# One vector instruction in place of three for the bias and the maximum of a softmax, on one Trainium2 core

## The chip, the core and the metric

The kernel runs on one core of one Trainium2 chip. TensorE (PE) multiplies matrices, VectorE (DVE) and ScalarE (ACT) work on tiles of 128 rows in the on-chip memory (SBUF) and in the eight accumulator banks (PSUM, named `ps` in the rows), GpSimd (POOL) has a small part, and SyncE (SP) starts the loads. Each engine runs its own list of instructions in order; semaphores tie the lists together. The metric is the device time of one execution in microseconds (us).

## The reference, cut to what matters

Two transformer-like blocks over 512 positions, width 1024, in float32. Four kinds of attention in it take a softmax over the scores of a query against its keys; everything else is projections, norms, a recurrence and two MLPs.

```python
def masked_softmax(s, mask):                       # first block, window and selected branches (NSA)
    s = jnp.where(mask, s.astype(jnp.float32), NEG_INF)
    m = jnp.max(s, axis=-1, keepdims=True)
    e = jnp.exp(s - m) * mask
    return e / jnp.maximum(jnp.sum(e, axis=-1, keepdims=True), 1e-30)
...
    s = jnp.einsum('bthd,bmhd->bhtm', q, mem_k) * (MEM_HEAD_DIM ** -0.5)   # memory heads, no mask
    prob = jax.nn.softmax(s.astype(jnp.float32), axis=-1)
```

The second block has differential attention (four heads of two score maps each, with a distance bias whose slope depends on the head), latent attention (four heads, called mla, block-causal mask) and, twice, cross attention to a memory of 256 rows (four heads, no mask). Each is softmax(scale * scores + bias) times values.

## The kernel before, in words

All activations lie transposed, 128 features by 512 positions. `dense` (L189) makes each product of a 128-column weight unit from three passes of float32r halves (`hi`, `lo`); ACT makes the high half of the next weights (`round_unit`, L165), DVE the low half (`rest_unit`, L171). That is most of PE's work.

The order on each engine is written out by hand: every stage is a set of generators, one for PE, one for DVE, one for ACT, and `weave` takes one step of each lane in turn. So the steps of different heads and of the dense products alternate in a fixed order on each engine.

A softmax head runs in steps of 128 queries, called items. In step n:
- PE makes the scores of item n into a bank (one for each of the item's one or two heads), the transposes of the probabilities of item n-1 (L157), and the product with the values of item n-2.
- DVE first finishes item n-1 (`head_vector`: reciprocal L382, gate L385, probabilities scaled L390), then prepares item n: the mask tile of 128 columns is added to the last 128 columns of the scores (L399), the row maximum over all nk columns is taken (L403), and it is multiplied by minus the scale (L406). Between these three DVE waits for its own last result.
- ACT takes the exponential with that column as bias, and sums the row (L421); it also copies the transposed probabilities (L432).

`nsa_heads`, `mem_heads`, `mla_head` and `cross_head` build such heads. NSA: 2 pairs of heads, 8 items each, nk = 128, 256, 384, 512 twice over, two heads in an item. Memory heads: 2 pairs, 4 items, nk = 256. mla: 4 heads, 4 items, nk = 128 to 512. Cross: 2 layers of 4 heads, 4 items, nk = 256. The mla and cross items have one score map each. Differential attention (`diff_vector`, `diff_scalar`) has code of its own: 4 heads, 4 items, two score maps in an item; the bias covers all nk columns, so one instruction for each map adds slope * 8 * dist to the scores (L1611), one takes the maximum (L1615), and one instruction scales both maxima (L1618). Its probabilities are finished by L1597, L1599, L1600 and L1603. The tiles are `db_...` and `dc_...` for its two lanes; lane A beside them runs the mla projections.

Every projection leaves its bank by `evac` (L273): times the row of reciprocal norms R, on DVE.

Of the kernel before, what the change touches and what calls it, by code (L numbers as in the profile page):

```python
# [268 lines left out]
def evac(K, M, v, key, dst, R, m=128):  # L269

    v.wait_ge(*K.done("pe", *key))
    v.wait_ge(*K.own("dve"))
    v.tensor_tensor(dst, K.bank(*key)[0:m, 0:dst.shape[1]], R, ALU.mult).then_inc(  # L273
        *K.tell("dve", *key, frees=key))
# [27 lines left out]
class Heads:  # L302


    def __init__(self, key, items, scale, ready, values, pr, pt, st, diag=None, first=True):
        self.key, self.items, self.scale, self.ready, self.values = key, items, scale, ready, values
        self.pr, self.pt, self.st, self.diag, self.first = pr, pt, st, diag, first
        self.heads = range(len(items[0].prods))
# [852 lines left out]
def nsa_vector(K, M, v):  # L1161
# [34 lines left out]
    weight_lo(K, M, v)  # L1196
    evac(K, M, v, ("gl",), s.tmp[0:12, :], R[0:12, :], 12)
# [70 lines left out]
def nsa_heads(M, z):  # L1268
# [6 lines left out]
    for br, k in enumerate((s.ks, s.kw)):  # L1275
        for i in range(4):
# [5 lines left out]
                 diag=M.C("causal"), first=False)  # L1282
# [64 lines left out]
def mem_heads(M, z):  # L1347
# [5 lines left out]
    return Heads(("memh", z), items, 0.125, [("dve", "mq", z)], [("act", *M0, "vt", 1)], s.pr, s.pt, s.st)  # L1353
# [230 lines left out]
def diff_vector(K, M, v, h, L):  # L1584
    k = ("df", h)
    for n, dst in (("q", L.q), ("k", L.k), ("v", L.sq)):
        project(K, M, v, (*k, n), dst)
        yield
    slope = 2.0 ** (-8.0 * (h + 1) / 4)
    if h < 2:  # L1590
        v.wait_ge(*K.landed("cs", 4))
    for step in range(6):
# [13 lines left out]
        if i < 4:  # L1606
            nk, st = (i + 1) * 128, L.st[i % 2]
            v.wait_ge(*K.done("pe", *k, "s", i, 1))
            for z in range(2):
                b = K.bank(*k, "s", i, z)  # L1610
                v.scalar_tensor_tensor(out=b[:, 0:nk], in0=M.even.dist(i), scalar=slope * 8.0, in1=b[:, 0:nk],  # L1611
                                       op0=ALU.mult, op1=ALU.add).then_inc(*K.tell("dve", *k, "bias", i, z))
            v.wait_ge(*K.own("dve"))
            for z in range(2):
                v.tensor_reduce(st[:, z:z + 1], K.bank(*k, "s", i, z)[:, 0:nk], AX, ALU.max).then_inc(  # L1615
                    *K.tell("dve", *k, "max", i, z))
            v.wait_ge(*K.own("dve"))
            v.tensor_scalar(st[:, 6:8], st[:, 0:2], -0.125, None, ALU.mult).then_inc(*K.tell("dve", *k, "nmax", i))  # L1618
# [11 lines left out]
def diff_scalar(K, M, a, h, L):  # L1630
# [5 lines left out]
    for step in range(6):  # L1636
        i = step
        if i < 4:
# [173 lines left out]
def mla_head(M, h, L):  # L1812
# [8 lines left out]
                 [("act", "ukv", h, "t")], [[x] for x in L.pr], [[x] for x in L.pt], L.st, diag=s.cm)  # L1821
# [31 lines left out]
def cross_head(M, n, h, L):  # L1853
# [3 lines left out]
    return Heads(("xh", n, h), items, 1.0 / 16, [("dve", "xq", n, h, 1), ("dve", "m", n + 1, "k", 2 * h + 1)],  # L1857
# [10 lines left out]
def queries_vector(K, M, v, n, h, fresh=None):  # L1868
    for z in range(2):
# [3 lines left out]
        evac(K, M, v, ("xq", n, h, z), M.Y[2 * h + z], M.R)  # L1873
# [356 lines left out]
def sync_program(K, M, s, dram):  # L2230

    load(K, s, "cst", M.pv, dram["pvec"])
    for n, (name, u) in enumerate(K.units):
# [27 lines left out]
        if (name, u) == ("w_out", 5):  # L2261
# [4 lines left out]
            load(K, s, "cs", M.even.cm, dram["cmask"])  # L2266
# [17 lines left out]
def build(nc, dram):  # L2284
    with ExitStack() as ctx:
# [48 lines left out]
        def pair_tiles(name, n, g_at, xf, s4, y, stats, after=None):  # L2334
# [25 lines left out]
                                          tile("cmp_w2", 42), tile("cmp_mask", 43))  # L2360
        s.q, s.qr = tiles("nsa_q", plain(1, 0), 2), tiles("nsa_qr", plain(1, 2), 2)
# [17 lines left out]
        s.cm = tile("cmask", 23)[:, 0:128]  # L2379
# [200 lines left out]
```

## Time and profile before

| what | us |
|---|---|
| median of 3 runs | 2209.06 (2205.78 to 2210.96) |
| the profiled execution, its time | 2210.41 |
| its span | 2209.1 |
| PE busy | 2049.4 |
| DVE busy | 1126.6 |
| ACT busy | 872.0 |

The span is the time from the first to the last instruction of the profile. Busy is the time in which an engine had at least one instruction under way, so two that overlap count once. The granted clock of PE over the span was 0.96 of full speed. The first block lies at 0 to 550 us (NSA and memory heads from 138 to 290), differential and latent attention from 555 to 780, the two cross layers around 845 to 965 and 1685 to 1803; the rest is dense work.

### The profile page before, as it was taken

What the parts mean: (1) busy time and instruction counts of PE and PEld (TensorE: products, weight loads), DVE (VectorE), ACT (ScalarE), POOL (GpSimd) and SP (SyncE); (2) the same over time, 40 slices, a digit from 0 to 9 for tenths busy, and PEclk for the clock granted to TensorE, in tenths of its full rate; (3) what the DMA queues carried; (4) which work ended last, traced back from release to release, by engine and by line L of the source; (5) the groups of instructions that cost most, each with busy time, mean ns of one, the idle gap of its engine ahead of it and who ended that gap; (6) DMA issues with size and microseconds to landing.
All of it is one profiled execution on the core that took longest, in us unless ns stands there. A gap on an engine that the chain in (4) does not pass through costs nothing.

```text
span 2209.1 us, 28369 instructions
## 1 busy us (share of the span) xinstructions
PE 2049.4 (93%) x11400; PEld 1622.4 (73%) x11400; DVE 1126.6 (51%) x2014; ACT 872.0 (39%) x1567; POOL 27.2 (1%) x68
## 2 busy tenths in 40 slices
PE   6888888899988999999999999999989999999997
PEld 5765666677756578978888887677567978888886
DVE  5666468737466455445343345344455445443344
ACT  5325443245343444434232233465644344232232
POOL 0000000000000000000000000011100000000000
PEclk9989899999989799999999999999999999999999
DMA  5210011012211023212222222111123312222321
GB/s 197 86 48 21 20 48 58 3 59 99 86 41 56 1 96 115 96 62 95 101 96 96 101 92 95 58 58 48 39 77 105 108 64 96 96 100 91 105 94 69
DMA packets 52051, 169.64 MB, mean 77 GB/s; under 512 B 5776, under 2 KB 9424, under 8 KB 51920
## 3 DMA queue, kind: packets, MB, share of 16 engines
q1 hardware_dynamic: 51920, 167.82, 21.7%
q8 instruction: 92, 1.51, 0.3%
q14 instruction: 39, 0.32, 0.0%
HBM read 165.70 MB, written 2.10 MB: 76 GB/s over the span
## 4 chain that ended last, share of the span: by engine, by line
PE 63%; DVE 3%; ACT 2%; issue 1%; POOL 0%; DVEq 0%; ACTq 0%
PE ps L152 62%; PE ps L157 1%; DVE X L1523 0%; DVE st L403 0%; DVE macc L233 0%; ACT sa_sp L2103 0%; DVE x_pr L390 0%; ACT sb_sp L2103 0%; ACT msq L226 0%; ACT sa_sp L2106 0%; ACT sa_sp L2101 0%; ACT sb_sp L2106 0%; ACT sb_sp L2101 0%; DVE lo L1431 0%; DVE st L1615 0%
## 5 line engine op out<-in xcount | busy, mean ns | idle before, releaser
L152 PE MATMUL ps<-hi,wr 128*128 128x512 f32 (+1 forms) x4616 | 1407.7, 385 | 50.7 <-DVE wr L171 34.3
L152 PEld LDWEIGHTS ps<-hi,wr 128*128 128x128 f32 x4616 | 862.4, 190 | 230.7 <-DVE wr L171 25.7
L152 PE MATMUL ps<-lo,wr 128*128 128x512 f32 (+1 forms) x2308 | 880.4, 381 | 0.0
L152 PEld LDWEIGHTS ps<-lo,wr 128*128 128x128 f32 x2308 | 440.0, 191 | 84.5 <-issue 3.9
L165 ACT ACTIVATE wr<-raw 128x1024 fp32r<-128x1024 f32 x293 | 307.7, 1052 | 349.3 <-PE ps L152 349.3
L171 DVE TENSOR_TENSOR wr<-raw,wr 128x1024 fp32r<-128x1024 f32 x293 | 356.7, 1217 | 4.3 <-ACT wr L165 2.3
L1450 DVE TENSOR_TENSOR X<-X,ps 128x512 f32<-128x512 f32 x96 | 66.0, 687 | 238.1 <-PE ps L152 238.1
L1986 ACT ACTIVATE mlp<-mlp 128x512 f32<-128x512 f32 x64 | 40.4, 632 | 207.8 <-DVE mlp L1969 207.8
L1969 DVE SCALAR_TENSOR_TENSOR mlp<-ps,R 128x512 f32<-128x512 f32 x64 | 44.2, 691 | 113.2 <-PE ps L152 106.2
L213 ACT ACTIVATE hi<-X,pv 128x512 fp32r<-128x512 f32 x48 | 34.7, 722 | 138.4 <-DVE X L1450 135.9
L1972 DVE TENSOR_TENSOR lo<-mlp,hi 128x512 fp32r<-128x512 f32 x64 | 44.3, 692 | 87.8 <-ACT hi L1990 87.8
L218 DVE SCALAR_TENSOR_TENSOR lo<-X,pv,hi 128x512 fp32r<-128x512 f32 x48 | 36.0, 751 | 40.7 <-ACT hi L213 40.7
L403 DVE TENSOR_REDUCE st<-ps 128x1 f32<-128x256 f32 (+3 forms) x96 | 41.7, 455 | 13.9 <-PE ps L152 10.1
L421 ACT ACTIVATE x_pr<-ps,st 128x256 f32<-128x256 f32 x32 | 15.2, 474 | 68.0 <-DVE st L406 68.0
L226 ACT ACTIVATE sq<-X 128x512 f32<-128x512 f32 x49 | 30.3, 619 | 28.9 <-DVE X L1450 28.9
L1990 ACT ACTIVATE hi<-mlp 128x512 fp32r<-128x512 f32 x64 | 40.4, 632 | 2.7 <-ACT mlp L1986 0.4
L233 DVE TENSOR_TENSOR acc<-acc,sq 128x512 f32<-128x512 f32 x50 | 34.6, 693 | 10.0 <-ACT sq L226 5.6
L273 DVE TENSOR_TENSOR Y<-ps,R 128x512 f32<-128x512 f32 x16 | 11.1, 691 | 54.3 <-PE ps L152 47.0
L152 PE MATMUL ps<-x_pt,vt 128*128 128x128 f32 x256 | 34.3, 277 | 2.9 <-ACT x_pt L432 2.9
L152 PEld LDWEIGHTS ps<-x_pt,vt 128*128 128x128 f32 x256 | 32.3, 191 | 5.4 <-ACT x_pt L432 4.6
L152 PE MATMUL ps<-sa_sp,cst 128*128 128x128 f32 (+3 forms) x84 | 27.3, 468 | 6.8 <-POOL sa_sp L2125 6.8
L152 PE MATMUL ps<-kt,Y 128*128 128x256 f32 x128 | 32.6, 379 | 0.0
(694 smaller groups left out, 1912.6 us busy)
## 6 DMA issues: line engine op xcount, KB each, us to landing
raw<-d_w SPq DMA_DIRECT2D x128, 512.0 KB, 3.4
raw<-d_wkv SPq DMA_DIRECT2D x32, 512.0 KB, 3.4
raw<-d_w_in SPq DMA_DIRECT2D x30, 512.0 KB, 3.5
raw<-d_sb_w_in SPq DMA_DIRECT2D x24, 512.0 KB, 3.4
raw<-d_ev_w_in SPq DMA_DIRECT2D x16, 512.0 KB, 3.5
raw<-d_wq SPq DMA_DIRECT2D x16, 512.0 KB, 3.4
raw<-d_wo SPq DMA_DIRECT2D x16, 512.0 KB, 3.5
X<-d_xT SPq DMA_DIRECT2D x16, 256.0 KB, 5.1
```

What stands on the lines that cost most here:

```text
L152: return pe.matmul(out, lhsT, rhs, start=start, stop=stop, skip_group_check=True)
L165: a.activation(M.wr[u % 3][:, 0:1024], M.raw[u % 4], ACT.Copy).then_inc(*K.tell("act", "hi", u))
L171: v.tensor_tensor(w[:, 1024:2048], M.raw[u % 4], w[:, 0:1024].bitcast(F32), ALU.subtract).then_inc(*K.tell("dve", "lo", u))
L213: a.activation(hi, src, ACT.Copy, scale=gcol).then_inc(*K.tell("act", *name, "hi", i))
L218: v.scalar_tensor_tensor(out=lo, in0=src, scalar=gcol, in1=hi.bitcast(F32), op0=ALU.mult, op1=ALU.subtract).then_inc(*K.tell("dve", *name, ...
L233: v.tensor_tensor(acc, acc, tmp[i % 2], ALU.add).then_inc(*K.tell("dve", *name, "sum", i))
L403: v.tensor_reduce(st[:, hh:hh + 1], K.bank(*h.key, "s", n, hh)[:, 0:nk], AX, ALU.max).then_inc(*K.tell("dve", *h.key, "max", n, hh))
L1450: v.tensor_tensor(M.X[u], M.X[u], K.bank(*key, u), ALU.add).then_inc(*K.tell("dve", *key, u, frees=(*key, u)))
L1969: v.scalar_tensor_tensor(out=t, in0=K.bank(*key), scalar=0.0, in1=M.R, op0=ALU.max, op1=ALU.mult).then_inc(*K.tell("dve", *key, frees=key))
L1972: v.tensor_tensor(lo[u], t, hi[u].bitcast(F32), ALU.subtract).then_inc(*K.tell("dve", "h", n, q, "lo", u))
L1986: a.activation(t, t, ACT.Square).then_inc(*K.tell("act", *key, "sq"))
L1990: a.activation(hi[u], t, ACT.Copy).then_inc(*K.tell("act", "h", n, q, "hi", u))
```

## The change

For masked and biased scores the three instructions become one call, `tensor_tensor_reduce`: it adds the mask to the scores, multiplies by minus the scale, writes that back to the bank, and gives the minimum of the row, which is the negated maximum of the scaled scores. The exponential then reads the bank with scale -1. The mask has to cover all nk columns, so the 128 columns of the mask get 384 columns of zeros in front. For NSA that tile is put where the rotation's cosines were, after their last use. In differential attention the slope is taken out of the bias: the queries leave their bank multiplied by 0.125 / slope, and the call scales by -slope. Where there is no mask, the maximum is taken with its sign turned, and the queries leave their bank already scaled.

```diff
-def evac(K, M, v, key, dst, R, m=128):
+def evac(K, M, v, key, dst, R, m=128, scale=None):
...
+    if scale is not None:
+        v.scalar_tensor_tensor(out=dst, in0=K.bank(*key)[0:m, 0:dst.shape[1]], scalar=scale, in1=R, op0=ALU.mult,
+                               op1=ALU.mult).then_inc(*K.tell("dve", *key, frees=key))
+        return
...
+def masked_max(K, v, b, mask, scale, nmax, *key):
+
+    v.tensor_tensor_reduce(out=b, in0=b, in1=mask, scale=-scale, scalar=3e38, op0=ALU.add, op1=ALU.min,
+                           accum_out=nmax).then_inc(*K.tell("dve", *key))
...
             for hh in h.heads:
-                b = K.bank(*h.key, "s", n, hh)
-                if h.diag is not None:
-                    v.tensor_tensor(b[:, nk - 128:nk], b[:, nk - 128:nk], h.diag, ALU.add).then_inc(
-                        *K.tell("dve", *h.key, "diag", n, hh))
-            v.wait_ge(*K.own("dve"))
-            for hh in h.heads:
-                v.tensor_reduce(st[:, hh:hh + 1], K.bank(*h.key, "s", n, hh)[:, 0:nk], AX, ALU.max).then_inc(
-                    *K.tell("dve", *h.key, "max", n, hh))
-            v.wait_ge(*K.own("dve"))
-            v.tensor_scalar(st[:, 2:2 + w], st[:, 0:w], -h.scale, None, ALU.mult).then_inc(
-                *K.tell("dve", *h.key, "nmax", n))
+                b, nmax = K.bank(*h.key, "s", n, hh)[:, 0:nk], st[:, 2 + hh:3 + hh]
+                if h.mask is not None:
+                    masked_max(K, v, b, h.mask[:, T - nk:T], h.scale, nmax, *h.key, "nmax", n)
+                else:
+                    v.tensor_reduce(nmax, b, AX, ALU.max, negate=True).then_inc(*K.tell("dve", *h.key, "nmax", n))
...
+    v.memset(s.mask[:, 0:384], 0.0).then_inc(*K.tell("dve", "mask0"))
+    v.tensor_copy(s.mask[:, 384:T], M.C("causal")).then_inc(*K.tell("dve", "mask"))
...
-    evac(K, M, v, ("mq", z), s.q, M.first.R)
+    evac(K, M, v, ("mq", z), s.q, M.first.R, scale=0.125)
...
             for z in range(2):
-                b = K.bank(*k, "s", i, z)
-                v.scalar_tensor_tensor(out=b[:, 0:nk], in0=M.even.dist(i), scalar=slope * 8.0, in1=b[:, 0:nk],
-                                       op0=ALU.mult, op1=ALU.add).then_inc(*K.tell("dve", *k, "bias", i, z))
-            v.wait_ge(*K.own("dve"))
-            for z in range(2):
-                v.tensor_reduce(st[:, z:z + 1], K.bank(*k, "s", i, z)[:, 0:nk], AX, ALU.max).then_inc(
-                    *K.tell("dve", *k, "max", i, z))
-            v.wait_ge(*K.own("dve"))
-            v.tensor_scalar(st[:, 6:8], st[:, 0:2], -0.125, None, ALU.mult).then_inc(*K.tell("dve", *k, "nmax", i))
+                masked_max(K, v, K.bank(*k, "s", i, z)[:, 0:nk], M.even.dist(i), slope, st[:, 6 + z:7 + z], *k, "nmax", i)
...
+    v.memset(s.cm[:, 0:384], 0.0).then_inc(*K.tell("dve", "cm0"))
```

On DVE, at the last item (nk = 512) of lane db in the second pair of differential heads, the order before was this. `ps` is a bank with scores, `dist_287` the distances, `st` the columns of statistics.

```order
L1611 SCALAR_TENSOR_TENSOR ps<-dist_287,ps 128x512 [waits s_pe]
L1611 SCALAR_TENSOR_TENSOR ps<-dist_287,ps 128x512
L1615 TENSOR_REDUCE st<-ps 128x1 [waits s_dve]
L1615 TENSOR_REDUCE st<-ps 128x1
L1618 TENSOR_SCALAR st<-st 128x2 [waits s_dve]
```

And now, with the finishing of the other lane's item behind it. An `ISA` row that reads a bank is the new instruction; the `ISA` row with one column behind it writes out the minimum that it gathered.

```order
L380 ISA ps,st<-ps,dist_287 128x512 [waits s_pe]
L380 ISA st 128x1
L380 ISA ps,st<-ps,dist_287 128x512
L380 ISA st 128x1
L1604 RECIPROCAL st<-st 128x2 [waits s_act]
L1606 TENSOR_TENSOR st<-st,omm 128x1 [waits s_dve]
L1607 TENSOR_SCALAR dc_pr_317<-dc_pr_317,st 128x384
L1610 SCALAR_TENSOR_TENSOR dc_pr_317<-dc_p_316,st,dc_pr_317 128x384 [waits s_dve]
```

Five instructions with two waits of DVE for itself became four without such a wait; what follows them, up to the probabilities that PE waits for, stands as it did.

At the first three mla items on DVE, with `cmask` as the mask tile, the order before was:

```order
L399 TENSOR_TENSOR ps<-ps,cmask 128x128 [waits s_pe]
L403 TENSOR_REDUCE st<-ps 128x1 [waits s_dve]
L406 TENSOR_SCALAR st<-st 128x1 [waits s_dve]
L399 TENSOR_TENSOR ps<-ps,cmask 128x128 [waits s_pe]
L403 TENSOR_REDUCE st<-ps 128x1 [waits s_dve]
L406 TENSOR_SCALAR st<-st 128x1 [waits s_dve]
```

And now:

```order
L380 ISA ps,st<-ps,cmask 128x128 [waits s_pe]
L380 ISA st 128x1
L380 ISA ps,st<-ps,cmask 128x128 [waits s_pe]
L380 ISA st 128x1
L380 ISA ps,st<-ps,cmask 128x128 [waits s_pe]
L380 ISA st 128x1
```

Three instructions became two. The order on PE is the same row for row, and on ACT too but for the line numbers. In the whole program there are 80 such pairs, 20 each of nk = 128, 256, 384 and 512.

## Rows read from the trace of the kernel before

**Rows 1.** The page: busy us of each engine, share, instructions.

```profile
PE 2049.4 (93%) x11400; PEld 1622.4 (73%) x11400; DVE 1126.6 (51%) x2014; ACT 872.0 (39%) x1567; POOL 27.2 (1%) x68
```

**Rows 2.** What PE waited for, 138 to 292 us: total us, times, longest.

```profile
PE ps L157 <- DVE mem_pr L390: 8.0, 5, 3.9
PE ps L152 <- ACT nsa_pta L432: 3.9, 2, 3.3
PE ps L157 <- DVE nsa_pra L390: 3.7, 4, 1.9
```

**Rows 3.** What PE waited for, whole span, same columns.

```profile
PE ps L157 <- DVE dc_pr L1603: 7.3, 7, 1.8
...
PE ps L157 <- DVE db_pr L1603: 4.5, 3, 2.8
...
PE ps L152 <- ACT x_pt L432: 2.9, 6, 0.5
...
PE ps L157 <- DVE mla_pr L390: 2.1, 3, 1.2
```

**Rows 4.** Groups by form, DVE: busy us, mean ns, idle before.

```profile
L1611 DVE SCALAR_TENSOR_TENSOR ps<-dist,ps 128x512 f32<-128x512 f32 x8 | 5.2, 690 | 1.7 <-PE ps L152 1.7
L273 DVE TENSOR_TENSOR Y<-ps,R 128x512 f32<-128x512 f32 x16 | 11.1, 691 | 54.3 <-PE ps L152 47.0 <-ACT R L256 7.0
```

**Rows 5.** Timeline of DVE, differential items nk = 128 and 512: start, us.

```profile
604.28 0.48 DVE L1611 SCALAR_TENSOR_TENSOR ps<-dist,ps 128x128 f32<-128x128 f32 x2
604.80 0.49 DVE L1615 TENSOR_REDUCE st<-ps 128x1 f32<-128x128 f32 x2
605.32 0.17 DVE L1618 TENSOR_SCALAR st<-st 128x2 f32<-128x2 f32 x1
...
708.79 1.29 DVE L1611 SCALAR_TENSOR_TENSOR ps<-dist,ps 128x512 f32<-128x512 f32 x2 [1.67 <-PE ps L152]
710.12 1.29 DVE L1615 TENSOR_REDUCE st<-ps 128x1 f32<-128x512 f32 x2
711.44 0.17 DVE L1618 TENSOR_SCALAR st<-st 128x2 f32<-128x2 f32 x1
```

**Rows 6.** The same view, an NSA item with nk = 512.

```profile
280.85 0.49 DVE L399 TENSOR_TENSOR ps<-ps,cst 128x128 f32<-128x128 f32 x2
281.37 1.29 DVE L403 TENSOR_REDUCE st<-ps 128x1 f32<-128x512 f32 x2
282.69 0.17 DVE L406 TENSOR_SCALAR st<-st 128x2 f32<-128x2 f32 x1
```

**Rows 7.** The same view, mla item nk = 128, and the next one's start.

```profile
727.26 0.29 DVE L399 TENSOR_TENSOR ps<-ps,cmask 128x128 f32<-128x128 f32 x1
...
727.99 0.29 DVE L399 TENSOR_TENSOR ps<-ps,cmask 128x128 f32<-128x128 f32 x1
```

**Rows 8.** Timeline of ACT: an exponential with its sum, and the next.

```profile
702.73 0.58 ACT L1646 ACTIVATE db_pr<-ps,st 128x384 f32<-128x384 f32 x1 [2.23 <-DVE st L1597]
703.20 0.19 ACT L1646 ACTIVATION_READ_ACCUMULATOR db_pr<-ps,st 128x1 f32 x1
703.30 0.57 ACT L1646 ACTIVATE db_p<-ps,st 128x384 f32<-128x384 f32 x1
```

**Rows 9.** Timeline of PE, waits (in brackets) in the first differential pair.

```profile
625.50 0.66 PE L157 MATMUL ps<-cst,db_pr 128*128 128x128 f32 x2 [2.82 <-DVE db_pr L1603]
...
637.95 0.52 PE L157 MATMUL ps<-cst,dc_pr 128*128 128x128 f32 x3 [1.75 <-DVE dc_pr L1603]
...
642.78 0.63 PE L157 MATMUL ps<-cst,db_pr 128*128 128x128 f32 x4 [2.26 <-DVE st L1597]
```

**Rows 10.** Stretches: us, busy PE PEld DVE ACT POOL, PE clock, DMA.

```profile
630.00:640.00 10.00, 7.63 (x36) 4.76 (x35) 9.72 (x22) 4.76 (x12) 0.00 (x0) 0.95 0.16 55
...
730.00:740.00 10.00, 10.00 (x21) 4.63 (x21) 5.02 (x20) 2.94 (x13) 0.00 (x0) 0.50 0.00 0
```

**Rows 11.** Groups by line: loads of ACT's function table.

```profile
L248 ACT ACT_TABLE_LOAD x7 | 9.0, 1283 | 2.5 <-PE ps L152 2.4
```

More of the change, by code:

```diff
@@ L302, with __init__ @@
 class Heads:
-    def __init__(self, key, items, scale, ready, values, pr, pt, st, diag=None, first=True):
+    def __init__(self, key, items, scale, ready, values, pr, pt, st, mask=None, first=True):
         self.key, self.items, self.scale, self.ready, self.values = key, items, scale, ready, values
-        self.pr, self.pt, self.st, self.diag, self.first = pr, pt, st, diag, first
+        self.pr, self.pt, self.st, self.mask, self.first = pr, pt, st, mask, first
         self.heads = range(len(items[0].prods))
@@ L421, in head_scalar @@
                 a.activation(h.place(h.pr, n, hh), K.bank(*h.key, "s", n, hh)[:, 0:nk], ACT.Exp,
-                             bias=st[:, 2 + hh:3 + hh], scale=h.scale, accum_out=st[:, 4 + hh:5 + hh]).then_inc(
+                             bias=st[:, 2 + hh:3 + hh], scale=1.0 if h.mask is None else -1.0, accum_out=st[:, 4 + hh:5 + hh]).then_inc(
                     *K.tell("act", *h.key, "e", n, hh, frees=(*h.key, "s", n, hh)))
@@ L1281, in nsa_heads @@
     return Heads(("nsa", z), items, 0.125, [("dve", "kw", "rope")], [("act", "vsw", "t")], s.pr, s.pt, s.st,
-                 diag=M.C("causal"), first=False)
+                 mask=s.mask, first=False)
 def nsa_heads_tensor(K, M, pe, z):
@@ L1352, in mem_heads @@
              for i in range(4)]
-    return Heads(("memh", z), items, 0.125, [("dve", "mq", z)], [("act", *M0, "vt", 1)], s.pr, s.pt, s.st)
+    return Heads(("memh", z), items, 1.0, [("dve", "mq", z)], [("act", *M0, "vt", 1)], s.pr, s.pt, s.st)
 def mem_heads_tensor(K, M, pe, z):
@@ L1524, in scale_vector, with project @@
                            op1=ALU.mult).then_inc(*K.tell("dve", *name, "x", i))
-def project(K, M, v, key, dst):
+def project(K, M, v, key, dst, scale=None):
     weight_lo(K, M, v)
@@ L1533, in project @@
         factors_vector(K, M, v)
-    evac(K, M, v, key, dst, M.R)
+    evac(K, M, v, key, dst, M.R, scale=scale)
 def diff_tensor(K, M, pe, h, L):
@@ L1585, in diff_vector @@
     k = ("df", h)
-    for n, dst in (("q", L.q), ("k", L.k), ("v", L.sq)):
-        project(K, M, v, (*k, n), dst)
+    slope = 2.0 ** (-8.0 * (h + 1) / 4)
+    for n, dst, scale in (("q", L.q, 0.125 / slope), ("k", L.k, None), ("v", L.sq, None)):
+        project(K, M, v, (*k, n), dst, scale)
         yield
-    slope = 2.0 ** (-8.0 * (h + 1) / 4)
     if h < 2:
@@ L1646, in diff_scalar @@
                 a.activation(pr[:, 0:nk], K.bank(*k, "s", i, z)[:, 0:nk], ACT.Exp, bias=st[:, 6 + z:7 + z],
-                             scale=0.125, accum_out=st[:, 2 + z:3 + z]).then_inc(
+                             scale=-1.0, accum_out=st[:, 2 + z:3 + z]).then_inc(
                     *K.tell("act", *k, "e", i, z, frees=(*k, "s", i, z)))
@@ L1820, in mla_head @@
     return Heads(("ml", h), items, 192.0 ** -0.5, [("act", "ukn", h), ("dve", "qrp", h // 2, "rope")],
-                 [("act", "ukv", h, "t")], [[x] for x in L.pr], [[x] for x in L.pt], L.st, diag=s.cm)
+                 [("act", "ukv", h, "t")], [[x] for x in L.pr], [[x] for x in L.pt], L.st, mask=s.cm)
 def mla_head_tensor(K, M, pe, h, L):
@@ L1856, in cross_head @@
                   [[(("xo", n, h, z), 0, lambda j, z=z: s.vap(j, 2 * h + z)) for z in range(2)]]) for i in range(4)]
-    return Heads(("xh", n, h), items, 1.0 / 16, [("dve", "xq", n, h, 1), ("dve", "m", n + 1, "k", 2 * h + 1)],
+    return Heads(("xh", n, h), items, 1.0, [("dve", "xq", n, h, 1), ("dve", "m", n + 1, "k", 2 * h + 1)],
                  [("act", "m", n + 1, "vt", 2 * h + 1)], [[x] for x in L.pr], [[x] for x in L.pt], L.st)
@@ L1872, in queries_vector @@
             v.wait_ge(*K.done("act", *fresh, "R"))
-        evac(K, M, v, ("xq", n, h, z), M.Y[2 * h + z], M.R)
+        evac(K, M, v, ("xq", n, h, z), M.Y[2 * h + z], M.R, scale=1.0 / 16)
 def queries_scalar(K, M, a, n, h, fresh=None):
@@ L2265, in sync_program @@
                 load(K, s, "cs", M.even.dist_t[j][:, 0:w], dram["dist"][:, j * T:j * T + w])
-            load(K, s, "cs", M.even.cm, dram["cmask"])
+            load(K, s, "cs", M.even.cm[:, 384:T], dram["cmask"])
             load(K, s, "mcs", M.even.cos, dram["mla_cos"])
@@ L2360, in build @@
                                           tile("cmp_w2", 42), tile("cmp_mask", 43))
+        s.mask = s.cos
         s.q, s.qr = tiles("nsa_q", plain(1, 0), 2), tiles("nsa_qr", plain(1, 2), 2)
@@ L2378, in build @@
         s.dist = lambda i: (d[0][:, 0:128], d[2][:, 0:256], d[0][:, 128:512], d[1])[i]
-        s.cm = tile("cmask", 23)[:, 0:128]
+        s.cm = tile("cmask", 23)
         s.cos, s.sin, s.kr, s.kn, s.vn = (tile("mla_cos", 24), tile("mla_sin", 25), tile("mla_kr", 26),
```

## The prediction

> **What bounds the kernel now.** I read the busy line of the page first, then what PE waited for, then DVE's timeline at those places. PE is busy 2049.4 of 2209.1 us, DVE 1126.6 [rows 1]. So DVE's time is worth nothing by itself; it counts where PE stands and waits for it, within some 160 us of idle PE in all. The reader is to look for waits that end at a softmax tile. In the stretch of NSA and memory heads these are `mem_pr` (8.0 us), `nsa_pra` (3.7) and, with ACT as the last link, `nsa_pta` (3.9) [rows 2]. In the differential and latent stages they are `dc_pr` (7.3), `db_pr` (4.5) and `mla_pr` (2.1); in cross attention only `x_pt` (2.9, six waits) [rows 3]. From 630 to 640 us DVE is busy 9.72 of 10 while PE is idle 2.4 [rows 10]: there DVE sets the pace.
>
> **The change on DVE, part by part.** The new instruction is in no row of before, so it is priced from its nearest relatives. The pass itself reads a bank and an SBUF tile and writes the bank, as L1611 does: 690 ns at 512 columns [rows 4]. Writing out the gathered minimum is a second instruction, as the order shows. ACT does the same kind of thing behind an exponential: the read-out takes 0.19, but it starts 0.47 after an activation of 0.58, and the next activation starts 0.57 after the first [rows 8]. So it costs the queue next to nothing between two passes, and its end comes 0.08 after the pass before it. I take a pass at its full length, and 0.08 once behind the last.
>
> Differential items (16). At nk = 512 the five instructions run from 708.79 to 711.61, 2.82 us [rows 5]. Two passes and a tail are 2 x 0.69 + 0.08 = 1.46: 1.36 less. At nk = 128 they run from 604.28 to 605.49, 1.21 [rows 5]; two passes of 0.29 and the tail are 0.66 (0.29 is the mask add of 128 columns, [rows 7]): 0.55 less. Four equally spaced sizes average 0.955, so 16 items give 15.3 us.
>
> NSA items (16). At nk = 512: 280.85 to 282.86, 2.01 [rows 6], against 1.46: 0.55 less. The mask add was 128 columns wide at every size, and is now as wide as the row, but rides in the pass of the maximum; so the difference is the same at every size: 8.8 us.
>
> mla items (16). From one item's start to the next one's at nk = 128 are 0.73 us [rows 7]; now 0.29 + 0.08 = 0.37. 0.36 less each: 5.8 us.
>
> Unmasked items (8 memory, 32 cross). The scaling of the maximum goes: 0.17 long in [rows 5, 6]. The next instruction can start before its end, as the second exponential does in [rows 8], so some 0.11 of it is queue time: 4.4 us for 40. A maximum with turned sign I take at the price of one without.
>
> Added: two memsets of 384 columns and a copy of 128. None can cost more than the 0.69 of a 512 column pass [rows 4], so at most 2.1; I take 1.0. The 22 projections that now multiply twice (4 differential, 2 memory, 16 cross queries) become the kind of instruction that L1611 is, 690 against 691 ns [rows 4]: nothing. The load of the mla mask moves the same bytes.
>
> Together DVE gets 15.3 + 8.8 + 5.8 + 4.4 - 1.0 = 33 us less to do.
>
> **What of it reaches the end.** Differential stage: DVE's order in a round is finish db, prepare db, finish dc, prepare dc. PE's wait for `dc_pr` stands behind the preparation of db in the same round, so it shrinks by up to 1.36: the wait of 1.75 at 637.95 falls to 0.4 [rows 9]. Then `db_pr` at 642.78 (2.26) stands behind the preparation of dc; it falls to about 0.9. The wait of 2.82 at 625.50 does not count: the projections for mla and their norm on ACT come directly before it on DVE. So of 7.3 + 4.5 + 2.3 = 14.1 us [rows 3, 9] 11.3 are open to the change, of which I take 80%, 9 us. Waits that end at ACT, in the same chains, give some 2 more. Sum 11, of 15.3 saved.
>
> NSA and memory stage: the three waits of [rows 2] sum to 15.6. PE steps of the recurrence lie between, and the memory items lose only their scaling. I take 5 of the 8.8 + 0.9, by the rule that DVE is busy somewhat over half of that stretch.
>
> mla: three items stand in a row behind each other from 727.26; 3 x 0.36 = 1.1. Then PE runs at half clock from 730 on, fully busy [rows 10], and hides the rest until near 758; the last head alone, where each item is a chain PE, DVE, ACT, DVE, PE, gives 4 to 5 x 0.36. Sum 3, near the 2.1 that PE waits for `mla_pr` and the ACT waits beside it.
>
> Cross: an exponential that starts some 0.15 earlier shortens a part of six waits of 2.9 in all: 0.7. The memsets and the copy: -0.5, where DVE is ahead of PE.
>
> Sum: 11 + 5 + 3 + 0.7 - 0.5 = 19 us. The profiled execution took 2210.4; it would be 2191. The median of before lies 1.3 lower, so the prediction is 2190.
>
> **The clock.** In [rows 10] PE's granted clock is 0.95 where it waits often but briefly and 0.50 (1.2 GHz) at 730 to 740, after waits at 700 to 730. Ten us at that level do the work of five. Shorter waits may keep such a stretch at 2.4 GHz, or the shifted waits may bring one down that was up. I hold one stretch of some 20 us either way for possible: 10 us. That gives the likeliest case its own range, 2180 to 2200.
>
> The Trainium skill, Vector Engine (DVE) Microarchitecture Reference, "Points that are easy to get wrong", warns of a related instruction: with two SBUF sources that aren't bf16 its rate is halved, since no read port is left for the accumulator. Here one source is a bank, so the rule as written would not strike; if it held for this instruction as well, the time would be that of the rival named half rate.
>
> **The rivals.**
>
> Half rate. If gathering the minimum takes a second cycle for each column, the length-dependent part of a pass doubles. From 0.29 and 0.69 at 128 and 512 columns a column costs 1.04 ns; passes become 0.42 and 1.22. A differential item is then 0.92 to 2.52 (0.3 less than before), an NSA item 0.92 to 2.52 against 1.23 to 2.01 (0.1 more on average), an mla item about equal. DVE saves 7 or 8 us, the path 3: 2206. For it: a gathered result is fed back each cycle; against it: L403 gathers too, at 1.29 for two passes of 512 [rows 6], the full rate. Chance 0.14.
>
> The gain goes elsewhere. ACT's exponentials and the recurrence's steps become the last link in most waits, so that only half of the 19 us arrives: 2200. For it: `nsa_pta` and the ACT waits [rows 2]; against it: the exponential itself waits for the column that now comes earlier. Chance 0.17.
>
> A fixed price for the new instruction. DVE has not run this operation before; if changing between it and the ordinary ones costs a setup, 80 pairs pay it. The nearest row is ACT's load of a function table, 1283 ns [rows 11]: 80 x 1.28 = 103 us more on DVE, 69 more net of the 33 saved, some 55% of it on the path: 2248. It breaks even at 33 / 80 = 0.42 us for each pair; from there on the kernel is slower than before. Against it: none of DVE's own operation changes in [rows 5 to 7] shows a gap over 0.04 us. Chance 0.06.
>
> It does what it says: the order shows the three instructions gone at all 88 items, so that is no rival.
>
> **How the numbers follow.** The forecast has 0.63 (2180 to 2200), the others 0.14, 0.17 and 0.06. The range reaches over the two small-gain cases to 2207, and down to 2179 for a clock that gains a whole stretch. A measurement of this kernel tells 0.2%, 4.4 us, from no change. Faster by more than that: the forecast nearly whole (0.61), the third case nearly whole (0.15), 0.03 of the half rate: 0.79. Within: 0.12, mostly half rate. Slower: 0.09, the fixed price and a clock that falls while the gain is small.
>
> **What would show it.** In the profile after: the new pass at 512 columns near 690 ns (1.2 us would be half rate; over 1.1 at 128 columns the fixed price); two passes and their read-outs at the place of 708.79 in some 1.5 us; DVE busy 1126.6 - 33 = 1094; waits for `dc_pr` and `db_pr` down from 11.8 to about 3; those for `mem_pr` almost as before; PE busy up or down with the clock alone. If DVE's busy time falls as said and the waits move to ACT rows, the third case was right. If the time falls by much more than 25 us, the clock did it, and a stretch such as 730 to 750 stands at 1.00.

## The result, and the profile after

| | median of 4 runs, us | range |
|---|---|---|
| before, run beside it | 2207.42 | 2205.06 to 2210.96 |
| after | 2168.78 | 2164.83 to 2172.61 |

The ratio is 0.9831, 95% interval 0.9808 to 0.9853: 38.6 us faster. The forecast was 19 us, and the range began at 2179. The direction was right, the size half of what came. Both profiled executions, before's and after's, took 3 to 4 us longer than their medians, so the two are fairly compared.

The page of after, its span and its busy line, answers to [rows 1]. The profiled execution took 2172.6.

```profile
span 2171.4 us, 28244 instructions
PE 2030.9 (94%) x11400; PEld 1613.2 (74%) x11400; DVE 1088.7 (50%) x1929; ACT 873.4 (40%) x1567; POOL 27.3 (1%) x68
```

The first thing to read here is a subtraction. PE idle was 2209.1 - 2049.4 = 159.7 and is 2171.4 - 2030.9 = 140.5: 19.2 us less, which is the sum of waits that was forecast. The other 18.5 us are PE's *busy* time, with the same 11400 instructions in the same order. What differs beside it is the granted clock, 0.960 over the span of before and 0.970 over that of after; that it is the cause is what the experiments have to show. DVE is 37.9 less busy (33 forecast); ACT stands as it was.

The groups of DVE by form, columns as in [rows 4]: the new instruction, its read-out, the maximum with turned sign, and the projection that now multiplies twice.

```profile
L412 DVE TENSOR_REDUCE st<-ps 128x1 f32<-128x256 f32 x48 | 19.6, 422 | 12.2 <-PE ps L152 11.9
L380 DVE DVE_READ_ACCUMULATOR2_ANT st<- 128x1 f32 x80 | 11.3, 142 | 0.0
L274 DVE SCALAR_TENSOR_TENSOR Y<-ps,R 128x512 f32<-128x512 f32 x16 | 11.1, 692 | 55.2 <-PE ps L152 47.9 <-ACT R L256 7.0
L380 DVE CUSTOM_DVE_ANT_0 ps<-ps,dist 128x512 f32<-128x512 f32 x8 | 5.4, 713 | 0.8 <-PE ps L152 0.8
...
L380 DVE CUSTOM_DVE_ANT_0 ps<-ps,dist 128x128 f32<-128x128 f32 x8 | 2.2, 315 | 1.1 <-PE ps L152 1.1
```

The pass takes 713 ns at 512 columns and 315 at 128, so 1.04 ns for a column, as an ordinary one, and some 25 ns more in all. There is no second cycle for a column (half rate would be 1220) and no fixed price (that would show at 128).

DVE's timeline at the place of 708.79 in [rows 5], the differential item with nk = 512:

```profile
686.03 0.70 DVE L380 CUSTOM_DVE_ANT_0 ps<-ps,dist 128x512 f32<-128x512 f32 x1 [0.76 <-PE ps L152]
686.65 0.14 DVE L380 DVE_READ_ACCUMULATOR2_ANT st<- 128x1 f32 x1
686.65 0.73 DVE L380 CUSTOM_DVE_ANT_0 ps<-ps,dist 128x512 f32<-128x512 f32 x1
687.30 0.14 DVE L380 DVE_READ_ACCUMULATOR2_ANT st<- 128x1 f32 x1
687.30 0.16 DVE L1604 RECIPROCAL st<-st 128x2 f32<-128x2 f32 x1
```

Each read-out starts together with the next instruction, so it takes nothing from the queue. The last column is there 687.44 - 686.03 = 1.41 us after the start (2.82 before, 1.46 forecast), and the next instruction starts after 1.27.

What PE waited for, whole span, columns as in [rows 2]:

```profile
PE ps L157 <- DVE mem_pr L401: 7.2, 3, 3.9
PE ps L157 <- DVE db_pr L1610: 3.7, 2, 2.6
PE ps L152 <- ACT nsa_pta L437: 3.5, 2, 2.7
PE ps L157 <- DVE nsa_pra L401: 2.9, 4, 1.2
...
PE ps L152 <- ACT x_pt L437: 2.6, 6, 0.5
PE ps L157 <- DVE dc_pr L1610: 2.5, 6, 0.7
```

Against [rows 2, 3], `dc_pr` fell from 7.3 to 2.5, and `db_pr` from 4.5 to 3.7. What is left of the latter is mostly the wait of 2.82 in [rows 9] that the prediction left out; it is on PE's timeline of after as

```profile
613.48 0.41 PE L157 MATMUL ps<-cst,db_pr 128*128 128x128 f32 x2 [2.64 <-DVE db_pr L1610]
```

**Where the other half came from.** Lined up by the 293 instructions of L171, one for each weight unit, after is ahead by 9.2 us at 300 us, 11.1 at 606, 17.1 at 649 and 39.5 at 784; from there to the end the lead stays between 37.5 and 40.2. So 22 us of the 38 were won in the second differential pair and in mla. The stretches there, columns as in [rows 10], before:

```profile
690.00:700.00 10.00, 7.13 (x38) 4.41 (x36) 8.20 (x33) 6.29 (x24) 0.00 (x0) 1.00 0.14 52
700.00:710.00 10.00, 7.43 (x27) 3.80 (x27) 7.69 (x20) 4.00 (x13) 0.00 (x0) 0.80 0.01 2
710.00:720.00 10.00, 8.25 (x47) 5.84 (x46) 8.22 (x21) 5.61 (x15) 0.00 (x0) 0.85 0.01 2
720.00:730.00 10.00, 8.83 (x47) 6.11 (x46) 5.30 (x16) 7.12 (x17) 0.00 (x0) 1.00 0.01 2
...
740.00:750.00 10.00, 10.00 (x19) 4.20 (x18) 2.94 (x10) 2.09 (x7) 0.00 (x0) 0.50 0.00 0
```

and after:

```profile
690.00:700.00 10.00, 9.51 (x62) 7.63 (x60) 4.43 (x10) 8.15 (x17) 0.00 (x0) 1.00 0.00 1
700.00:710.00 10.00, 10.00 (x40) 5.23 (x40) 6.19 (x27) 5.70 (x21) 0.00 (x0) 1.00 0.01 2
710.00:720.00 10.00, 10.00 (x37) 4.41 (x35) 4.15 (x16) 4.21 (x12) 0.00 (x0) 1.00 0.00 1
720.00:730.00 10.00, 9.79 (x73) 8.32 (x72) 3.59 (x14) 5.64 (x13) 0.00 (x0) 1.00 0.01 2
```

Two more stretches belong here, first of before and then of after, in the first differential pair:

```profile
620.00:630.00 10.00, 6.91 (x19) 3.49 (x19) 6.91 (x18) 4.22 (x13) 0.00 (x0) 0.50 0.00 1
```

```profile
620.00:630.00 10.00, 8.87 (x57) 6.95 (x56) 8.06 (x23) 5.95 (x14) 0.00 (x0) 1.00 0.03 9
```

The reader is to see the long stretch at 0.50 (1.2 GHz) in the first table, 20 us with PE 10.00 busy, together with its 730 to 740 in [rows 10], and that the same latent products at 700 to 720 of after stand at 1.00. On PE's timelines one pair of them, first before, then after:

```profile
735.04 1.49 PE L152 MATMUL ps<-mla_kn,Y 128*128 128x384 f32 x2
```

```profile
705.90 0.81 PE L152 MATMUL ps<-mla_kn,Y 128*128 128x384 f32 x2
```

### The profile page after: what moved, and what is told of

Same layout as the page of the kernel before. It is cut to its first block, busy times and chain, and to the rows that moved or that the text cites. A ratio compares the mean times of both kernels' runs of the same rounds, so it can differ in the third digit from the quotient of the medians.

```text
span 2171.4 us, 28244 instructions
## 1 busy us (share of the span) xinstructions
PE 2030.9 (94%) x11400; PEld 1613.2 (74%) x11400; DVE 1088.7 (50%) x1929; ACT 873.4 (40%) x1567; POOL 27.3 (1%) x68
## 4 chain that ended last, share of the span: by engine, by line
PE 85%; DVE 9%; ACT 4%; issue 1%; DMA 0%; POOL 0%; SPq 0%; DVEq 0%; ACTq 0%
PE ps L152 83%; PE ps L157 3%; DVE ps L380 1%; DVE wr L171 1%; DVE X L1530 0%; DVE lo L218 0%; DMA cst<-d_cst 0%; DVE macc L233 0%; DVE ra_S L769 0%; DVE rc_S L769 0%; DVE rb_S L769 0%; DVE ra_Z L789 0%; ACT sa_sp L2103 0%; DVE x_acc L233 0%; ACT wr L165 0%
## 5 line engine op out<-in xcount | busy, mean ns | idle before, releaser
L171 DVE TENSOR_TENSOR wr<-raw,wr 128x1024 fp32r<-128x1024 f32 x293 | 356.7, 1217 | 4.3 <-ACT wr L165 2.3
L274 DVE SCALAR_TENSOR_TENSOR Y<-ps,R 128x512 f32<-128x512 f32 x16 | 11.1, 692 | 55.2 <-PE ps L152 47.9
L152 PEld LDWEIGHTS ps<-x_pt,vt 128*128 128x128 f32 x256 | 32.3, 191 | 5.2 <-ACT x_pt L437 4.3
L152 PE MATMUL ps<-sb_sp,cst 128*128 128x128 f32 (+3 forms) x84 | 26.8, 455 | 7.5 <-POOL sb_sp L2125 7.5
```

The lines of the kernel that those rows point to most:

```text
L152: return pe.matmul(out, lhsT, rhs, start=start, stop=stop, skip_group_check=True)
L171: v.tensor_tensor(w[:, 1024:2048], M.raw[u % 4], w[:, 0:1024].bitcast(F32), ALU.subtract).then_inc(*K.tell("dve", "lo", u))
```

## The experiments

Each kernel is told as a difference from before or after. A is the theory that the clock gave the half that was not forecast, because PE stood for shorter times ahead of it; what the other letters stand for is in the expectations. "Gain" is the difference of medians to before, run on the same chip: 2206.81 for the first four, 2206.56 for the next four, 2208.98 for the last four. PE idle and PE busy are those of one profiled execution.

| kernel | median (range, runs) | ratio (95%) | gain | PE idle | PE busy |
|---|---|---|---|---|---|
| before | | | | 159.7 | 2049.4 |
| e1_diff_only | 2190.36 (2179.75 to 2199.63, 6) | 0.9925 (0.9897 to 0.9954) | 16.5 | 148.1 | 2039.2 |
| e2_nsa_only | 2200.06 (2194.36 to 2202.51, 11) | 0.9966 (0.9954 to 0.9979) | 6.8 | 155.3 | 2039.8 |
| e3_mla_only | 2195.32 (2193.41 to 2199.28, 5) | 0.9952 (0.9934 to 0.9970) | 11.5 | 155.7 | 2036.4 |
| e4_plain_only | 2209.65 (2201.64 to 2213.25, 12) | 1.0013 (0.9999 to 1.0026) | -2.8 | 155.7 | 2044.7 |
| e5_warm_before | 2201.12 (2195.61 to 2203.36, 8) | 0.9968 (0.9956 to 0.9981) | 5.4 | 157.4 | 2036.9 |
| e6_late_pair | 2173.79 (2172.25 to 2179.91, 4) | 0.9857 (0.9840 to 0.9874) | 32.8 | 144.0 | 2028.3 |
| e7_no_mla | 2174.29 (2168.86 to 2189.17, 6) | 0.9868 (0.9844 to 0.9891) | 32.3 | 143.5 | 2024.1 |
| e9_after_warm | 2167.91 (2166.70 to 2169.73, 4) | 0.9826 (0.9811 to 0.9840) | 38.7 | 133.7 | 2031.8 |
| e10_no_diff | 2189.13 (2181.92 to 2190.47, 5) | 0.9909 (0.9894 to 0.9924) | 19.9 | 152.4 | 2028.3 |
| e11_no_nsa | 2180.24 (2177.32 to 2183.03, 4) | 0.9871 (0.9856 to 0.9886) | 28.7 | 143.1 | 2036.6 |
| e12_masked_only | 2171.63 (2168.30 to 2175.57, 4) | 0.9833 (0.9815 to 0.9851) | 37.4 | 141.0 | 2033.3 |
| e13_after_again | 2169.97 (2165.78 to 2174.12, 4) | 0.9825 (0.9807 to 0.9843) | 39.0 | 139.0 | 2033.9 |

The last two columns need care. The profiled execution was the fastest of its kernel in e3, e4, e5, e7, e9 and e10, by up to 8 us below the median (e4, 2201.64), and that of before was a slow one. What such a pair differs by over the whole span is therefore partly chance. It is safer to compare a stage with the same stage. These are the lengths of three stages in each profile, cut at the same instructions of L171 (which stand at 123, 298, 590, 649, 689 and 784 us in before), and for the third its PE idle time and its granted clock:

| kernel | NSA and memory | first differential pair | second pair and mla | PE idle in it | clock in it |
|---|---|---|---|---|---|
| before | 174.4 | 58.9 | 95.4 | 13.6 | 0.82 |
| e2_nsa_only | 163.0 | 58.9 | 95.4 | 13.6 | 0.82 |
| e4_plain_only | 171.1 | 59.0 | 89.6 | 13.5 | 0.87 |
| e1_diff_only | 174.3 | 51.9 | 76.8 | 8.5 | 0.95 |
| e7_no_mla | 162.6 | 51.3 | 76.7 | 8.5 | 0.95 |
| e3_mla_only | 172.8 | 58.9 | 81.5 | 11.3 | 0.94 |
| e10_no_diff | 160.1 | 58.4 | 81.5 | 11.2 | 0.94 |
| e5_warm_before | 170.4 | 58.9 | 86.3 | 11.3 | 0.94 |
| e6_late_pair | 162.8 | 51.4 | 81.5 | 10.3 | 0.92 |
| after | 165.2 | 51.9 | 73.0 | 6.0 | 0.97 |
| e13_after_again | 162.7 | 52.0 | 74.6 | 6.0 | 0.96 |
| e12_masked_only | 163.9 | 52.1 | 74.5 | 6.0 | 0.96 |
| e11_no_nsa | 173.4 | 52.4 | 73.0 | 6.0 | 0.98 |
| e9_after_warm | 163.9 | 51.6 | 73.0 | 6.0 | 0.98 |

The rest, from 784 us to 2150, takes 1364.8 to 1369.6 in all of them, 1366.1 in before and 1367.8 in after: nothing was won there.

### Each part alone

The edit is before, with the changed lines taken over for one of four parts: differential heads, NSA heads, mla heads, or the heads without a mask ("plain": memory and cross).

```diff
-NEW = ()
+NEW = ("diff",)      # e1; e2 ("nsa",), e3 ("mla",), e4 ("plain",)
```

> Of the change only the differential heads (16 items, scaled queries for them); all other softmaxes as before. Theory A (the waits of PE got shorter by the 19 us forecast, and because PE stood less, its granted clock stayed at 2.4 GHz in stretches where it had been at 1.2, which gave another 19): this part holds the stretch before latent attention, where most of the clock was lost, so it gives 10 us in waits and 10 to 14 in clock, 20 to 25 us less than before, and the half-clock stretch that lay at 730 to 754 us is gone or much shorter. Rival B (every us saved on DVE brings its share, whatever the place: 38.6 us in all for 33 us of DVE): 15.3 us of DVE give 18 less.

> Of the change only the NSA heads (16 items) with their wide mask. A: 8 to 9 us less than before, 4 of it in waits and 4 to 5 in clock (half-clock stretches between 240 and 290 us shorter); nothing later changes. B: 8.8 us of DVE give 10 less. The two hardly differ here; the share of PE busy time in it does: 4 or 5 us less busy by A, none by B.

> Of the change only the latent attention heads (16 items). A: the waits before 730 us stay as they were, so PE still falls to 1.2 GHz there and hides what DVE saves up to 754 us; 2 to 3 us less than before. B: 5.8 us of DVE give 7 less.

> Of the change only the unmasked heads (memory and cross, 40 items): maximum with turned sign, no scaling behind it, scaled queries. A: 0 to 2 us less, since cross attention waits little. B: 4.4 us of DVE give 5 less.

PE idle fell by 11.6, 4.4, 4.0 and 4.0 over the whole span. In the stages that a part changes it fell by 10.8 (e1, both pairs), 4.5 (e2) and 2.3 (e3), against the terms 11, 5 and 3 of the sum. The plain part was forecast at 0.7, and its median shows no gain at all. The gains in time are uneven: 16.5, 6.8, 11.5 and -2.8, in all 32 of the 38. B, a fixed price for each us of DVE, had said 18, 10, 7 and 5; A had said 20 to 25, 8 to 9, 2 to 3 and 0 to 2. Neither fits: 5.6 us less on DVE brought 11.5 (e3), and 7.4 less brought nothing (e4).

mla alone is the surprise: 11.5 us for a term of 3. Its stretches, columns as above:

```profile
700.00:710.00 10.00, 8.50 (x26) 4.18 (x27) 8.05 (x20) 4.53 (x16) 0.00 (x0) 0.66 0.00 0
...
730.00:740.00 10.00, 10.00 (x39) 4.79 (x40) 4.56 (x17) 4.00 (x12) 0.00 (x0) 1.00 0.00 0
740.00:750.00 10.00, 10.00 (x75) 8.24 (x74) 3.20 (x12) 5.84 (x12) 0.00 (x0) 1.00 0.01 2
```

The differential waits up to 710 are still there. The 0.66 at 700 to 710 is the short stretch that before shows as 0.80 and 0.85 from 700 to 720, since e3 runs 3.3 us ahead here. But 730 to 750 now stands at 1.00 instead of 0.50. One wait ahead of it is gone. It is this one, on PE's timeline of before, at the first mla item, directly where its stretch at 0.50 begins:

```profile
717.17 0.63 PE L157 MATMUL ps<-cst,db_pr 128*128 128x128 f32 x4 [1.40 <-ACT dc_p L1646]
718.84 0.63 PE L157 MATMUL ps<-cst,dc_pr 128*128 128x128 f32 x4 [0.35 <-DVE dc_pr L1603]
729.96 0.47 PE L157 MATMUL ps<-cst,mla_pr 128*128 128x128 f32 x1 [1.17 <-DVE mla_pr L390]
```

In e3 the first two are as they were, and no wait stands at the third. In e1 it is the other way round: the wait of 1.40 is gone, the two of 1.6 for `dc_pr` ahead of it are under 0.5, and the third stands, with 1.00 behind it:

```profile
714.31 0.33 PE L158 MATMUL ps<-cst,mla_pr 128*128 128x128 f32 x1 [1.17 <-DVE mla_pr L402]
```

Over all kernels the pattern is this. Where the wait of 1.17 and the differential waits ahead of it both stand (before, e2, e4), the latent products run partly or wholly at a lower level: 0.50 twice over in before and in e2 (720 to 740), 0.74 in e4. Where the differential waits are shorter and the 1.17 stands (e1, e7), or the other way round (e3, e10, e6), or both are short (after and the rest), or the waits are filled (e5), they stand at 1.00: eleven profiles of fourteen. So either part saves this stretch, and both save it once. The stage from 689 to 784 gives the size: the differential part alone shortens it by 18.6 us, mla alone by 13.8, both together by 22.3. The 10.1 us by which the two exceed the whole are what can be won only once. The size is not fixed, though: e4 changes nothing in this stage, has the same waits as before, and came out 5.8 us shorter, with 0.74 in place of 0.50. The expectation of 2 to 3 us under A was wrong, though the means is A's: it had counted the clock for the differential part alone.

### Products that only keep PE busy, in the kernel before

No line of DVE is touched. Where PE would stand and wait for probabilities, it first makes products of a constant tile, whose result nobody reads: 8, 8, 6 and 6 of them at four places (the first two items of the differential head 3, the last item of head 2, and the first mla item). They are work added to the kernel, 28 products of 128 columns, which the trace shows as two instructions each.

```diff
+def warm(M, pe, b, n):
+    for _ in range(n):
+        mm(pe, b[:, 0:128], M.C("ones"), M.C("ones"), True, True)
...
+            warm(M, pe, b, {(3, 0): 8, (3, 1): 8, (2, 3): 6}.get((h, i), 0))
```

> The kernel before, with 28 extra products of 128x128 on PE, whose results nothing reads, where PE waits for probabilities between 692 and 730 us (heads 2 and 3 of differential attention, first item of latent attention). No vector or scalar instruction changes. A (the clock): PE keeps 2.4 GHz where it had 1.2 at 706 to 713 and 730 to 754 us, that is 31 us at half speed less, so the time falls by 10 to 15 us to 2192 to 2197, minus 1 or 2 for products that don't fit into the waits, and PE's instructions of the old kinds there take less time in all. C (the gain beyond the waits is something else, such as less traffic of DVE on the banks): the half-clock stretch may move, but the time stays or rises by 1 to 4 us.

It is 5.4 us *faster* than before, ratio 0.9968 (0.9956 to 0.9981), where C had said the same or slower and A 10 to 15 faster. The granted clock rose with it: on average 0.967 over its eight executions, 0.962 over the thirteen of before beside them. One of the four places on PE's timeline, and the stretches:

```profile
720.63 1.60 PE L152 MATMUL ps<-cst 128*128 128x128 f32 x12
```

```profile
700.00:710.00 10.00, 7.50 (x48) 5.56 (x47) 9.02 (x22) 5.05 (x14) 0.00 (x0) 1.00 0.00 1
710.00:720.00 10.00, 10.00 (x61) 7.68 (x59) 3.98 (x9) 7.04 (x13) 0.00 (x0) 1.00 0.01 2
...
730.00:740.00 10.00, 10.00 (x40) 4.91 (x40) 5.84 (x18) 4.13 (x12) 0.00 (x0) 1.00 0.01 2
740.00:750.00 10.00, 9.08 (x67) 7.49 (x65) 4.07 (x16) 5.20 (x11) 0.00 (x0) 1.00 0.00 0
750.00:760.00 10.00, 7.72 (x31) 4.90 (x31) 3.83 (x13) 3.43 (x10) 0.00 (x0) 0.81 0.00 0
```

DVE does as much as before (1127.0 busy), PE does more, and 730 to 750 stands at 1.00. The place in the row above is that of the wait of 1.17. This is the run that shows the clock as a cause by itself. Over the whole span PE is busy 12.5 us less, but this was the fastest execution of the eight, and 7.9 us of its lead were there at 590 us, before the first filler. The stage with the fillers is the fair measure: 86.3 us instead of 95.4, so 9.0 shorter, 2.3 of it in idle time and 6.7 in PE busy, though the fillers themselves are busy for 7.3. Part of the 9.0 is lost again later, and the clock falls in another place instead (0.81 at 750 to 760).

### Giving back some of DVE's time, in the kernel after

After the new instruction, in the second pair of differential heads alone, DVE waits for itself once and reads both rows again; the result goes to a column that nobody reads.

```diff
                 masked_max(K, v, K.bank(*k, "s", i, z)[:, 0:nk], M.even.dist(i), slope, st[:, 6 + z:7 + z], *k, "nmax", i)
+            if h >= 2:
+                v.wait_ge(*K.own("dve"))
+                for z in range(2):
+                    v.tensor_reduce(st[:, z:z + 1], K.bank(*k, "s", i, z)[:, 0:nk], AX, ALU.max).then_inc(
+                        *K.tell("dve", *k, "nmax", i))
```

> The changed kernel, with DVE's old time put back in the second pair of differential heads alone: after the new instruction it waits for itself and takes the maximum of both maps again, 2.8 us an item at 512 columns as before, before ACT may go on. A: the waits of 690 to 720 come back, 5 or 6 us, and with them part of the half-clock stretch; since latent attention keeps its shorter items, between 5 and 18 us slower than the changed kernel, and the profile's half-clock time at 660 to 770 says which. B (each us of DVE counts alike): 7.7 us of DVE bring 9 us back.

It is 5.0 us slower than after (2173.79 against 2168.78; 5.8 when each is taken against its own before), which is at the low end of what A said and below what B said. DVE's timeline at one such item shows that the delay was really there:

```profile
686.21 0.73 DVE L380 CUSTOM_DVE_ANT_0 ps<-ps,dist 128x512 f32<-128x512 f32 x1
686.86 0.14 DVE L380 DVE_READ_ACCUMULATOR2_ANT st<- 128x1 f32 x1
687.03 1.29 DVE L1621 TENSOR_REDUCE st<-ps 128x1 f32<-128x512 f32 x2
```

DVE is 7.4 busier and PE idle 3.5 more. PE busy over the whole span is not more (2028.3 against 2030.9), but that hides what happened in the stage itself:

```profile
670.00:680.00 10.00, 7.63 (x30) 4.25 (x28) 7.88 (x30) 4.82 (x18) 0.00 (x0) 0.83 0.01 2
680.00:690.00 10.00, 8.41 (x24) 4.12 (x25) 8.09 (x23) 4.69 (x16) 0.00 (x0) 0.66 0.00 0
```

In after both stretches stand at 1.00. So behind the lengthened waits the clock did fall, for some 10 us, and the stage takes 81.5 instead of 73.0, half of the difference in idle and half in busy time. What did not come back is the long stretch in the latent products, which stand at 1.00 from 700 to 730: mla's wait of 1.17 is still gone here. The other stages of this profile happened to run faster than after's, so the total doesn't tell A from B.

### Each part left out of the kernel after

```diff
-NEW = ("nsa", "mla", "diff", "plain")
+NEW = ("nsa", "diff", "plain")      # e7; e10 without "diff", e11 without "nsa", e12 without "plain"
```

> The changed kernel with latent attention as before. Alone that part brought 11 us. A: the half-clock stretch at 730 us goes as soon as either the differential part or this one shortens the waits before it, so its 10 us are counted once; without this part the changed kernel loses only its waits, 3 to 5 us. B (the parts add up): it loses 11 us, or 17 with the 6 us by which the four parts alone fell short of the whole.

> The changed kernel with the differential heads as before. A (19 us of waits, the rest from PE's clock, which a stretch gives back once): this part holds 10 to 12 us of waits, plus the clock of its own two stages, less what latent attention alone keeps up at 730 us; 14 to 20 us slower than the changed kernel. B (time goes with DVE's work): 15.3 of 33 us, 18 slower.

> The changed kernel with the NSA heads as before. Alone the part brought 6 to 7 us, 3 of it in waits. Its stage lies 300 us ahead of the others, so nothing is shared with them. A: 6 to 9 us slower than the changed kernel. B: 10.

> The changed kernel with the unmasked heads as before. Alone that part made the kernel 3 us slower, within its spread, by clock and not by waits. A: the clock of single stretches falls one way or the other with shifts of less than a us, so 3 us to either side of the changed kernel. D (scaled queries and the sign turned cost something): 3 us or more faster than it. B: 5 slower.

> The changed kernel itself once more, beside the three that leave out a part, for direct comparison: 36 to 40 us less than before, and a spread of its runs of 5 to 8 us that goes with their mean granted clock.

The median of after is 2169.97 in the last of these, 2168.78 in its first measurement. Against the one on the same chip, leaving out the differential part costs 19.2 us, NSA 10.3, the plain part 1.7; leaving out mla costs 5.5 against 2168.78. The sum is 37. So mla is worth 11.5 alone and 5.5 as the last one in (6.3 when e7 and after are each taken against their own before): the stretch at 730 to 750 can be saved once, by it or by the differential part, as the pattern above says. A had said 3 to 5, B 11. One of e7's six executions took 2189.17, at a granted clock of 0.961 where the others have 0.969 or more. The 19.2 fits both theories. NSA goes the other way, 6.8 alone and 10.3 as the last one in, nearer to B's 10 than to A's 6 to 9; its stage takes 160.1 to 165.2 us with the change and 170.4 to 174.4 without, so it is worth some 10 us with 4 or 5 us of chance about it. The plain part can't be told from nothing in either setting.

### Filler products in the kernel after

The same helper, with 62 products at seven waits that were left: 36 at three memory items, 6 at an NSA item, 20 at three items of the first differential pair.

```diff
+            warm(M, pe, b, {(0, 1): 10, (0, 0): 6, (1, 0): 4}.get((h, i), 0))
```

> The changed kernel with extra 128x128 products on PE in waits of its own: memory heads items 0 to 2 of the first pair (36), the first item of the second NSA pair (6), first items of differential heads 0 and 1 (20). A: the half-clock stretches at 143 to 160, 249 to 259 and 593 to 617 us shrink, 5 to 10 us less than the changed kernel. C: 0 to 5 us slower, since products that outlast a wait are paid for.

At 2167.91 it is 0.9 below one measurement of after and 2.1 below the other, inside what two measurements of after differ by (1.2) and their ranges. PE idle fell by 6.8, and PE busy rose by 0.9 against the first profile. A had said 5 to 10 us faster, C the same or slower. The granted clock did rise, to 0.977 on average over the four executions from 0.972 over the eight of after, and the time stayed: the fillers, busy for 15.6 us, cost about what their clock gives. No version clearly beats the changed kernel.

## Why the prediction was half right

- **The price of the pass** (0.69, with 0.08 behind the last): right; 0.71, and the item of 512 columns takes 1.41 instead of 1.46. DVE's saving of 33 us was 37.9. By the parts alone (e1 to e4) DVE's busy time fell by 15.0, 8.3, 5.6 and 7.4, against 15.3, 8.8, 5.8 and 4.4: the term that was too small is that of the unmasked items, whose scaling of 0.17 was counted at 0.11. A smaller thing is the overlap of the new passes. The first mla items follow each other on DVE's timeline like this, 0.21 to 0.25 apart and not 0.37:

```profile
701.64 0.29 DVE L380 CUSTOM_DVE_ANT_0 ps<-ps,cmask 128x128 f32<-128x128 f32 x1
701.85 0.14 DVE L380 DVE_READ_ACCUMULATOR2_ANT st<- 128x1 f32 x1
701.85 0.33 DVE L380 CUSTOM_DVE_ANT_0 ps<-ps,cmask 128x128 f32<-128x128 f32 x1
702.10 0.14 DVE L380 DVE_READ_ACCUMULATOR2_ANT st<- 128x1 f32 x1
```

- **What of it reaches the end** (11 + 5 + 3 + 0.7 - 0.5 = 19): right in the sum, 19.2 of PE idle, and in its parts where they were run alone, 10.8, 4.5 and 2.3 in their own stages. `dc_pr` and `db_pr` came to 6.2 and not "about 3", because that number had forgotten the wait of 2.8 at 625.50 that the prediction itself had set aside. Without it they are 3.6.
- **The clock** (one stretch of some 20 us either way, so 10 us either way around nothing): this is the step that failed. PE's busy time fell by 18.5 us, and 14.8 of them lie in the second differential pair and mla. Three things were wrong. It was treated as chance, with zero as its middle, though the waits that the prediction shortened lay among stretches below 1.00, and none of its steps lengthened one. It was sized by the one stretch that was looked at: 730 to 750 is gone, worth 10 us (the overlap of the two parts in that stage), but the shorter stretches ahead of it, 0.80 and 0.85 at 700 to 720, are gone too, and 620 to 630 of before was at 0.50, while in after no stretch from 610 to 640 is below 0.80. And the term for mla, 3, was reckoned with the half clock left standing, so that it would hide what DVE saves; with the stretch gone the part brought 13.8 us in its stage. That the sign was certain is not shown either: e4 too only takes work from DVE, and its clock is 0.960 on average over twelve executions, with 0.962 for before.
- **Half rate**: refuted by 713 ns at 512 columns. The Trainium skill's sentence on this (Vector Engine (DVE) Microarchitecture Reference, "Points that are easy to get wrong") speaks of two SBUF sources; with one source in a bank the full rate was measured, so the trace agrees with its wording, and it does not carry over.
- **The gain goes elsewhere**: refuted; ACT's waits fell too (`nsa_pta` 3.9 to 3.5, `x_pt` 2.9 to 2.6), and half of the saved DVE time arrived as reckoned.
- **A fixed price**: refuted by 315 ns at 128 columns.

The prediction did name its own error: "If the time falls by much more than 25 us, the clock did it, and a stretch such as 730 to 750 stands at 1.00." That is what came.

What stays open: why the clock rises or falls just where it does. The wait of 1.17 is followed by 0.50 in before and by 1.00 in e1, and before and e4 have the same waits from 690 to 730 to within 0.05 us and unequal levels behind them. Executions of one kernel differ by 3 to 20 us along with their mean granted clock (e1: 2179.75 at 0.969, 2199.63 at 0.960). So the split of a single profile between idle and clock carries some microseconds of that. That the clock is worth about half of the gain rests on two profiles of after, which have PE busy 18.5 and 15.5 below before's, and on e5 for the cause. All executions together allow an estimate that comes out lower: a straight line through 45 executions of before (2199.91 to 2213.82 us at 0.966 to 0.958) falls by 1.3 us for each 0.001 of clock, and after's eight have 0.972 on average where before's have 0.962, so some 13 of the 38.6 us. Why the two differ isn't shown. In the NSA stage nothing was filled, so there the clock's part is argued and not shown.

## What to carry to other kernels

Where PE waits often and briefly, read the granted clock in the stretches behind the waits before summing them: a busy stretch at 0.50 behind waits may go when they get shorter, and a change that shortens them deserves a clock term that leans to the faster side, here between a third and a half of the gain. Read it stage by stage, not from the whole span of two single profiles: kernels with the same instructions in a stage agreed there within 1.6 us in the two later stages, with one exception of 5.8, and within 5 or so in the NSA stage. Fusing an add, a scale and a row maximum into one pass was worth up to 1.4 us an item (2.82 to 1.41 at 512 columns) where DVE was the last link, since it makes one pass out of two and takes away DVE's waits for itself. Run the parts alone and left out: where the two differ (11.5 and 5.5 for mla), look for something that two parts share and that can be won once.

## What the runs showed of the hardware

Products that nobody reads can make a kernel faster: 28 of them took 5.4 us off 2206.56. The read-out of a gathered minimum on DVE takes 142 ns and none of the queue; on ACT it took 0.19 [rows 8]. And one wait of 1.17 us on PE, taken away (e3) or filled (one of four fills in e5), went with some 20 us at 2.4 GHz in place of 1.2; with the waits ahead of it shortened instead (e1), it did no harm.
